# A four-layer fp32 model on one core, with the rounded activation tiles moved to another place within 1024 bytes of SBUF

## The reference, cut to what matters

```python
m = (g[:, :, 0] * (y_hg @ w_br_hg) + g[:, :, 1] * (y_gla @ w_br_gla)
     + g[:, :, 2] * (y_nsa @ w_br_nsa))
x = x + m @ w_out
x = x + (silu(h @ w_gate) * (h @ w_up)) @ w_down
```

```python
hid = silu(einsum('td,edf->tef', t, w1)) * einsum('td,edf->tef', t, w3)
y = einsum('tef,efd->td', hid * combine[:, :, None], w2)
```

## The kernel before, in words

| tile | byte | past a multiple of 1024 |
|---|---|---|
| high, low (the weights) | 32896, 49280 | 128 |
| hh, hl | 77184, 85376 | 384 |
| ffn_high, ffn_low | 125120, 147648 | 192 |
| early_high/low (start, ffn) | 170496, 178688; 182784, 190976 | 512 |
| cat_high, cat_low | 155584, 163776 | 960 |
| z_high, z_low | 122816, 139200 | 960 |
| hidden_high_half, hidden_low_half | 134208, 142400 | 64 |
| combine_high, combine_low, eye | 123840, 124864, 125888 | 960 |

## Time and profile before

### The profile page before, as it was taken

One profiled execution on the slowest core, in us unless ns is written; L12 is line 12 of the kernel. 1 busy time (PEld: TensorE's weight loads), 2 busy tenths in 40 slices (PEclk: granted clock), 3 DMA queues, 4 the chain that ended last, 5 costly groups with the idle time before them and its releaser, 6 DMA issues. The chain is left out here.

```text
span 2356.1 us, 40120 instructions
## 1 busy us (share of the span) xinstructions
PE 2113.6 (90%) x16870; PEld 2009.8 (85%) x16870; DVE 1458.5 (62%) x2361; ACT 1043.2 (44%) x1462; POOL 0.2 (0%) x4
## 2 busy tenths in 40 slices
PE   6977798999989787999996878999969998799997
PEld 6977777999988786799996768999969777799997
DVE  5956555687577664657854565777759655465554
ACT  5643343544464433445443334444455554344443
POOL 0000000000000000000000000000000000000000
PEclk8988898999989897999998988999979988899999
DMA  5323313588534232246964324687725312355552
GB/s 191 127 98 91 125 65 108 178 298 277 176 126 135 84 114 66 96 144 224 319 214 136 124 90 143 240 296 287 272 98 167 125 64 72 113 174 177 181 175 94
DMA packets 101411, 370.15 MB, mean 157 GB/s; under 512 B 11632, under 2 KB 11888, under 8 KB 100976
## 3 DMA queue, kind: packets, MB, share of 16 engines
q1 hardware_dynamic: 100080, 364.25, 46.1%
q10 hardware_dynamic: 1152, 3.33, 0.4%
HBM read 366.50 MB, written 1.05 MB: 156 GB/s over the span
## 5 line engine op out<-in xcount | busy, mean ns | idle before, releaser
L297 DVE TENSOR_TENSOR low<-raw,high 128x1024 fp32r<-128x1024 f32 x590 | 719.5, 1222 | 493.4 <-ACT high L294 492.4
L294 ACT CAST high<-raw 128x1024 fp32r<-128x1024 f32 x590 | 613.7, 1045 | 590.0 <-PE ps L362 546.1
L360 PE MATMUL ps<-hh,high 128*128 128x256 f32 x2832 | 832.4, 294 | 26.1 <-PEq L591 11.2
L361 PE MATMUL ps<-hh,low 128*128 128x256 f32 x2832 | 818.4, 289 | 0.0
L362 PE MATMUL ps<-hl,high 128*128 128x256 f32 x2832 | 817.4, 289 | 0.0
L360 PEld LDWEIGHTS ps<-hh,high 128*128 128x128 f32 x2832 | 561.8, 198 | 45.5 <-issue 38.9
L361 PEld LDWEIGHTS ps<-hh,low 128*128 128x128 f32 x2832 | 561.9, 198 | 0.5 <-issue 0.5
L362 PEld LDWEIGHTS ps<-hl,high 128*128 128x128 f32 x2832 | 561.0, 198 | 0.0
L360 PE MATMUL ps<-ffn_high,high 128*128 128x256 f32 x672 | 189.6, 282 | 2.2 <-DVE ffn_low L1877 2.2
L361 PE MATMUL ps<-ffn_high,low 128*128 128x256 f32 x672 | 187.3, 279 | 0.0
L362 PE MATMUL ps<-ffn_low,high 128*128 128x256 f32 x672 | 187.2, 279 | 0.0
(11 more groups left out here) (428 smaller groups left out, 2835.1 us busy)
## 6 DMA issues: line engine op xcount, KB each, us to landing
raw<-in_stream SPq DMA_DIRECT2D x590, 512.0 KB, 4.0
ada_rows<-in_ada SPq DMA_DIRECT2D x96, 512.0 KB, 5.5
c_act<-in_c SPq DMA_DIRECT2D x3, 512.0 KB, 4.2
bias<-in_bias ACTq DMA_DIRECT2D x1, 1536.0 KB, 6.5
xT<-in_xT SPq DMA_DIRECT2D x4, 256.0 KB, 5.8
out<-xT SPq DMA_DIRECT2D x1, 1024.0 KB, 3.9
par<-in_par SPq DMA_DIRECT2D x1, 858.0 KB, 4.9
hybrid_const<-in_const ACTq DMA_DIRECT2D x1, 800.0 KB, 6.0
```

Source lines behind the costliest of these rows:

```text
L294: return act.copy(self.high[:, slot, :], self.raw[:, slot, :])
L297: return dve.tensor_tensor(self.low[:, slot, :], self.raw[:, slot, :], self.high[:, slot, :].bitcast(F32), ALU.subtract)
L360: pe.matmul(out, sh, mh, start=start, stop=False, **more)
L361: pe.matmul(out, sl, mh, start=False, stop=False, **more)
```

## The change

Before an fp32r tile other than `high` and `low` is taken, a filler is taken that brings the tile to 64 bytes past the next multiple of 1024. `nc.sbuf_base` is the next free byte.

```diff
+STEP, PLACE = 1024, 64
...
         def sb(name, shape, scope=everywhere, dt=F32):
 
+            if dt == F32R and name not in ("high", "low"):
+                ahead = (PLACE - nc.sbuf_base) % STEP
+                if ahead:
+                    scope.enter_context(nc.sbuf_tensor("ahead_of_" + name, [P, ahead // 4], F32))
             tile = scope.enter_context(nc.sbuf_tensor(name, shape, dt))
```

## The result

The kernel after takes **2329.6 us** (median of four runs, 2324.9 to 2331.6) against 2363.5 for the kernel before: ratio 0.9855, interval 0.9836 to 0.9875. That is 34 us less, inside the range of 2297 to 2342, but 18.6 us short of the forecast 2311. The profiled execution took 2324.9 us, 33.0 less than that of before.

What follows compares the result with a forecast made beforehand. TensorE's own pace was taken to bound the long product runs. Stage gains of 45.0 us plus 9 from mixers and gates made 54, taking the 2364.5 us median to 2310.5, stated as 2311; range 2297 to 2342.

Steps and rivals of the forecast that it cites:

- the case that I held likeliest: Whole kernel: the gain comes as forecast, about 54 us, spanning 2297 to 2320 us; chance 0.52.
- rival 1: Long hh runs enter at 117.8 ns and stay: 2320 to 2340 us in part (0.28), 2356 wholly (0.09).
- The mechanism: Rounded matmuls: the start of each moving slice sets the spacing, 120 ns at even multiples of 64, 113.4 or 117.8 at odd.
- I take 113.4 ns for every rounded moving tile at 64: All rounded moving tiles: 113.4 ns from start to start, as hidden has from its fourth matmul on; hh had 120.0.
- Gate and up: 1728 matmuls on hh in two layers: 11.4 us gained, 8.8 kept after 1.3 lost per layer to VectorE's row loop.
- Experts: Two mixtures of experts, 3072 matmuls on hh: 20.3 us gained, 20 kept, since VectorE can follow.
- Mamba projection: Dense part, 31 of 48 units, 744 matmuls at 6.6 ns each: 4.9 us gained, 4 kept.
- All the rest: Projection 2.5 us, down products 3.5, mix 1.7, early halves 3.4, z_high and cat_high 1.1, mixers and gates 9.
- The token-major products: 576 matmuls where only the stationary side moves: taken as 0, bounds 0 and -3.8 us, or as much lost.
- Rival 2: Products: other traffic or output bank order, not the byte, parts 120 from 113.4; no change, 2364.5 us; chance 0.06.
- Rival 3: Mixers: longer TensorE waits lower the granted clock below 0.88, more matmuls run at 1.2 GHz, kernel slower; chance 0.05.
- Plain matmuls: 2,902 unrounded fp32 matmuls, on sq, W, seg and others, also shift: cost taken as 0, up to 18 us possible.

Runs made afterwards that it cites:

- after_again: The kernel after, unchanged, run and profiled a second time; 2330.9 us.
- hh_only: The kernel before with only hh and hl moved, from 384 to 64, all other tiles keeping their places modulo 1024; 2326.7 us, ratio 0.9849.
- weights_192: The kernel before with only the weights' halves high and low moved, from 128 to 192 past a multiple of 1024; 2344.7 us, ratio 0.9918.
- three_rows_before: The kernel before with three row buffers for ada_w in place of two, all places as before; 2360.0 us, ratio 0.9989.
- low_even: The kernel after with the weights' low half moved to 64, 0 from the moving tiles, high staying 64 from them; 2356.2 us, one run.

## Why the prediction was right, and where it was short

The number lies in the range, but not by the case that I held likeliest (2297 to 2320 us): rival 1 came true in part.

- **The mechanism** held: the place of the moving tiles sets the spacing, and no instruction is needed for it. I had read it as the tile's own place; it is the distance to the weights. As the weights did not move, both readings gave the same forecast.
- **The step that was mis-sized** is "I take 113.4 ns for every rounded moving tile at 64". It is 115.3 on `hh` in the profiled execution, 114.7 in `after_again`. This was rival 1, at 0.28 for a part, with 2320 to 2340 us. I argued that 64 "has never shown 117.8" before. In the trace of before `hidden` is always entered from `hh` at 120.0; that it came out at 113.3 each time said nothing about entry from elsewhere. It was also the only tile at 192 modulo 256 from the weights; `ffn_high`, `z_high` and `cat_high` were at 64.
- **Gate and up**: kept 8.8 us, measured 5.6. In the first layer VectorE's loop cost 97.7 - 95.8 = 1.9 us where I had 1.3, part of it by the change to 117.8 behind the wait; in the second it cost nothing, because the run was at 117.8, slow enough for the rows.
- **Experts**: 20 forecast, 13.0 measured, because a third of the products there, and `hidden` with them, are at 117.8. This is not bad luck: it is the same in four profiles. `hh_only` gained 19.8 us there, so 20 was right for moving `hh`, and the forecast put the side effect of the other tiles' places at nothing.
- **Mamba projection**: 4 forecast, 1.4 measured. Its last 288 matmuls, with the wait behind them, took 40.6 us before, 40.5 at 117.8, and 40.7 in `hh_only` at 113.3, where the wait had grown from 5.8 to 7.8 us. The next step on TensorE waits for something else, so nothing of these products' gain got through.
- **All the rest** (projection, down products, mix, early halves, `z_high`, mixers): 21.2 forecast, 13.0 measured. The first layer's down product stayed at 117.8, so its 2.3 us never came. The token-major products, for which I took 0, went from 119.9 to some 116 ns.
- **Rival 2**, no effect of the byte, is excluded by `weights_192`: `hh` at 384, where it was, runs at 113.3. The Trainium skill's rule that the moving side and LDWEIGHTS read through ports of their own and TensorE waits for nobody (SBUF — State Buffer, Who interferes with whom) does not carry over to what two such streams cost together: here moving the weights changed the pace of the products on every tile. The floor that the Trainium skill gives (TensorE: Matmul & The Clock Gate, "Wait — 56ns, not 53.3ns?"), an estimate of 109.2 ns for 256 columns, was not reached by the rounded products of any run.
- **Rival 3**, the clock: 0.926 before, 0.923 after. In the mixers' stretch it was 0.87 against 0.88, the sign that I had named, but small: 466 matmuls on `hh` ran at 1.2 GHz in place of 418, which is at most 4.8 us at 100 ns each. `three_rows_before`, with the old spacing, had 465, so this need not be the change's doing.
- **Plain matmuls**: no cost showed. Four on `sq` still start 215 to 216 ns apart, and 1765 distances between plain matmuls at the full clock sum to 152.3 us before and 152.6 after.

## What to carry to other kernels

Where TensorE loads a new stationary tile for each matmul, read the distance from start to start, not the busy time, and compare tiles by their byte offset from the weights: here an odd multiple of 64 was worth up to 5.6%, and 8 bytes beside it nothing. Move the tile that matters first, and alone: moving all of them lost 7 us in the experts that moving `hh` alone did not, and was no faster over the whole kernel. When a part gets faster, look for the loop that ran just level with it: a third buffer, worthless before, took 1.4 to 1.9 us off one stage once the products were quicker.

## What the runs showed of the hardware that was not expected

- For 128x256 fp32r products with a load before each, at the full granted clock, the spacing depended on (moving start less weights' start) modulo 128: 64 gave 113.3 or 117.8 ns; 0 gave 118.6 or 120.0; 96 gave 118.3; 48, 80, 56, 72 and 32 gave 117.5 to 121.1.
- The choice between the two spacings of one distance differed in gate and up between two profiles of the same program, lasted through hundreds of matmuls, and could change where a run was broken by a wait or by other matmuls. In the experts it was the same, expert by expert, in four profiles on at least three chips, and changed when other tiles than those of the products were moved (`hh_only`).
- At 64 modulo 256 the narrow spacing was rarer than at 192: 15 to 19% against 44 to 67% of the matmuls on `ffn_high`.
- With the low half of one side at an even distance and the others at an odd one, the narrow spacing did not occur on `hh`; 122.1 did in `low_even`.

What decides the choice at the start of a run stays open, and so does which tile's place changes it in the experts. That it is a conflict of the two reads of SBUF is an inference from the distance rule; no run looked at the reads themselves.
